# Gate products spread among the steps of an attention, wide products in four more stages, convolution taps moved, weights stored by block

## What is computed

```python
# block 1
z = rms(x, g) @ w_in;  q, k, v, u = split(z)
m = concat(chunked_attention(q, k, v, rel_bias), pool(u)) @ w_o
x = x + rms(m, g2)
up = causal_conv3(rms(x, g3) @ w_up)                   # 2 x 5632 channels, 3 taps
x = x + rms((gelu(up[:5632]) * up[5632:]) @ w_down, g4)
# block 2, with a context of 256 tokens and a condition c
s1, b1, a1, s2, b2, a2 = split(silu(c) @ w_ada + b_ada)   # also for the context
h = rms(x) * (1 + b1) + s1                             # the context the same way
k_a, v_a, k_b, v_b = kv(h and context);  q_a, q_b, g_a, g_b = h @ w_in_2
o_a = attention of 16 heads (4 key heads), q and k normed and rotated
o_b = rms over each of 8 heads of (softmax(q1 k1) - lam * softmax(q2 k2)) v
x = x + a1 * ((sigmoid(g_a) * (o_a @ w_br_a) + sigmoid(g_b) * (o_b @ w_br_b)) @ w_out)
x = x + a2 * ((silu(h2 @ w_ff_gate) * (h2 @ w_ff_up)) @ w_ff_down)
```

## Time and profile before

| | |
|---|---|
| median of 3 runs | 3146.78 us (3143.88 to 3147.21) |
| profiled execution, its own time | 3145.76 us |
| its span, first to last instruction | 3143.9 us |
| granted TensorE clock, mean | 0.97 |
| busy: TensorE, VectorE, ScalarE, GpSimd | 93%, 62%, 50%, 25% |
| weight loads | 1120 of 512 KB, 4.8 us to landing in most stages |
| moved | 598 MB, 190 GB/s over the span |

### The profile page before, as it was taken

How to read it: one execution, slowest core, us unless ns; L and a number is a source line. 1 busy time by engine, 2 the same in 40 slices (tenths; PEclk the granted TensorE clock), 3 DMA queues, 4 the chain that set the end, 5 groups by cost and what they waited for, 6 DMA issues and landing times.

```text
span 3143.9 us, 57610 instructions
## 1 busy us (share of the span) xinstructions
PE 2926.2 (93%) x20282; PEld 2699.2 (86%) x20282; DVE 1946.6 (62%) x2412; ACT 1564.1 (50%) x2203; POOL 786.3 (25%) x646
## 2 busy tenths in 40 slices
PE   7998789999998997999998778999997999999999
PEld 7988789999988997788898547999996888888888
DVE  5566888776688866433456555655766665555554
ACT  5555554345565543323455645665535644334443
POOL 2554432003233321212341402445303400000000
PEclk9999899999999998999998989999998999999999
DMA  7874666657777764344574003887755865656655
GB/s 245 266 246 126 222 201 201 180 181 243 240 225 227 235 218 148 120 149 135 180 248 140 1 1 125 255 261 247 241 182 178 255 213 181 188 186 187 187 185 163
DMA packets 595176, 598.29 MB, mean 190 GB/s; under 512 B 18257, under 2 KB 593105, under 8 KB 594833
## 3 DMA queue, kind: packets, MB, share of 16 engines
q1 hardware_dynamic: 591936, 589.37, 60.3%
q10 hardware_dynamic: 2368, 4.91, 0.4%
q0 software_dynamic: 784, 2.88, 0.3%
HBM read 594.99 MB, written 2.10 MB: 190 GB/s over the span
## 4 chain that ended last, share of the span: by engine, by line
PE 60%; DVE 15%; DMA 10%; ACT 7%; issue 7%; DVEq 1%; ACTq 0%; SPq 0%
PE acc L1334 19%; PE acc L1330 13%; PE acc L1332 13%; PE acc L1333 12%; DVE wlo L850 5%; DMA raw<-w_ada 5%; DMA raw<-w_in 2%; ACT whi L540 2%; ACT cond_products L536 1%; DVE cond_sums L842 1%; DVE conv_out L936 1%; PE sums L1392 1%; DMA raw<-w_up 1%; DMA raw<-w_brb 1%; DVE conv_in L924 1%
## 5 line engine op out<-in xcount | busy, mean ns | idle before, releaser
L850 DVE TENSOR_TENSOR wlo<-raw,whi 128x1024 fp32r<-128x1024 f32 x864 | 1120.3, 1307 | 892.5 <-ACT whi L540 888.9
L1334 PE MATMUL acc<-operand,wlo 128*128 128x256 f32 (+1 forms) x5504 | 1606.6, 292 | 0.0
L540 ACT ACTIVATE whi<-raw 128x1024 fp32r<-128x1024 f32 x864 | 911.3, 1058 | 1096.5 <-PE acc L1334 733.5
L1332 PE MATMUL acc<-operand,whi 128*128 128x256 f32 (+1 forms) x4096 | 1222.6, 298 | 98.3 <-DVE wlo L850 63.4
L1333 PE MATMUL acc<-operand,whi 128*128 128x256 f32 (+1 forms) x4096 | 1210.7, 296 | 0.0
L1334 PEld LDWEIGHTS acc<-operand,wlo 128*128 128x128 f32 x5504 | 1063.0, 193 | 15.4
L1332 PEld LDWEIGHTS acc<-operand,whi 128*128 128x128 f32 x4096 | 795.4, 194 | 125.4 <-DVE wlo L850 56.5
L1333 PEld LDWEIGHTS acc<-operand,whi 128*128 128x128 f32 x4096 | 795.6, 194 | 15.0
L408 POOL TENSOR_TENSOR cond_products<-cond_products 128x512 f32<-128x512 f32 x192 | 252.6, 1316 | 1425.9 <-ACT cond_products L536 1424.0
L1330 PE MATMUL acc<-operand,whi 128*128 128x512 f32 x1408 | 502.9, 402 | 16.9 <-DVE wlo L850 9.0
L536 ACT ACTIVATE cond_products<-raw,cond_silu 128x256 f32<-128x256 f32 x768 | 327.8, 498 | 255.7 <-PE acc L1334 159.3
(11 more groups left out here) (201 smaller groups left out, 2000.0 us busy)
## 6 DMA issues: line engine op xcount, KB each, us to landing
raw<-w_ada SPq DMA_DIRECT2D x256, 512.0 KB, 4.7
raw<-w_in SPq DMA_DIRECT2D x224, 512.0 KB, 4.8
raw<-w_up SPq DMA_DIRECT2D x176, 512.0 KB, 4.8
raw<-w_down SPq DMA_DIRECT2D x88, 512.0 KB, 4.9
raw<-w_fg SPq DMA_DIRECT2D x88, 512.0 KB, 4.3
raw<-w_fu SPq DMA_DIRECT2D x88, 512.0 KB, 4.5
raw<-w_fd SPq DMA_DIRECT2D x88, 512.0 KB, 3.5
raw<-w_o SPq DMA_DIRECT2D x32, 512.0 KB, 4.8
```

Of the source, the lines that this page charges most:

```text
L540: act.activation(whi[j % RING][:], raw[j % RING][:], ACT.Copy).then_inc(hi_done, 2 if st.entries[j % st.upb - 1] == (None, ADA_VEC) else 1)
L850: dve.tensor_tensor(wlo[j % RING][:], raw[j % RING][:], whi[j % RING][:].bitcast(F32), ALU.subtract).then_inc(lo_done, 2 if prev[0] is Non ...
L1332: pe.matmul(out_, h[:, x, f], mov[:, 0], start=first, stop=False)
L1334: ins = pe.matmul(out_, l[:, x, f], mov[:, 0], start=False, stop=last)
```

## The change

It has five parts.

1. **Gates among the attention.** The two gate stages become one, `gates`, of 64 units without items. The norms, attention A and attention B are cut into steps, and slot s of 64 holds gate unit s and the steps due there: norms in slots 0 to 9, attention A from slot 11 (`AT_A`), B from slot 43 (`AT_B`). ScalarE and VectorE prepare unit s+4 in slot s. A gate group accumulates in one bank (`PS[:, 0, gb % 2]`); the other two banks are left to the scores, so that A keeps two score buffers and B, whose step fills both, has one. Sigmoids go to a staging buffer `GT` (in the place of the condition sums), are stored to HBM (`spill`), and are loaded back ahead of the branch stages. The sums and the root of B's output norm move into `branch_a`, behind its first unit, with `output_norm`.
2. **Items** move: `up1b` (split in two, `up1b` and `up1c`) and `out` get four each, the gates none.
3. **Wide form** also in `mix_out`, `down1`, `down2` and `q` stages. In three of them ScalarE first copies the low half into `tiles` (`low_half`), VectorE then adds the high half; in `down2` VectorE adds both.
4. **Convolution.** The newest tap goes to ScalarE (`newest_tap`, Identity with scale and bias from a column), the older ones to `older_taps`, which runs behind the next split.
5. **Layout.** The host stores each matrix by blocks of 256 columns (`by_block`), so that a unit's 4 KB per partition lie in a row.

```diff
-V_STEPS = {"scale": 0, "mix_out": 3, "conv": (6, 9), "down1": 0, "down2": 3, "kv": 0, "q": 0, "gate": 0,
+V_STEPS = {"scale": 0, "mix_out": 3, "conv": (4, 7), "down1": 0, "down2": 4, "kv": 0, "q": 0, "gate": 0,
-A_STEPS = {"conv": (1, 0), "gate": (1, 1), "glu": (2, 1)}
-WIDE = ("glu", "down_x")
+A_STEPS = {"conv": (2, 1), "glu": (2, 1), "mix_out": 1, "down1": 1, "q": 1}
+WIDE = ("glu", "down_x", "mix_out", "down1", "down2", "q")
+LOW_FIRST = ("mix_out", "down1", "q")
...
+    def block_of(w, g, k):
+        return W[w][:, ds(g, 1), k:k + UK, :].rearrange("p g k c -> p (g k) c")
...
-    st_up1b = Stage("up1b", pairs("w_up", "w_up", 4 * GW, DFF + 4 * GW), 2 * n1 - 8, 4, "conv", tile0=8, feat0=8)
+    st_up1b = Stage("up1b", pairs("w_up", "w_up", 4 * GW, DFF + 4 * GW), 8, 4, "conv", ada=1, tile0=8, feat0=8)
+    st_up1c = Stage("up1c", pairs("w_up", "w_up", 8 * GW, DFF + 8 * GW), 2 * n1 - 16, 4, "conv", tile0=16, feat0=16)
-    st_ga = Stage("gate_a", cols("w_in2", 0, KVW + QW, GW), 8, 4, "gate", ada=1, tile0=16)
-    st_gb = Stage("gate_b", cols("w_in2", 0, KVW + QW + D, GW), 8, 4, "gate", ada=1, tile0=48)
+    st_g = Stage("gates", cols("w_in2", 0, KVW + QW, GW), 16, 4, "gate")
-    st_out = Stage("out", cols("out", 0, 0, GW), 8, 4, "out", op=104)
+    st_out = Stage("out", cols("out", 0, 0, GW), 8, 4, "out", ada=1, op=104)
...
+        GT = sb("gate_out", [P, 2, S], F32, place["at"] - 2 * GW * 4)
+        gates = nc.dram_tensor("gates_spilled", (P, 32, S), F32).ap()
+        AT_A, AT_B = 11, 43
...
+            pool.wait_ge(gate_out, 16 * 16)
+            for st in (st_ba, st_bb, st_out, st_u1a):
                 add_condition(st)
...
+            def low_half(st, b, gb):
+                tile = b * (2 * st.GB) + (st.tile0 + 2 * gb)
+                act.wait_ge(used, grouped(st, b, gb))
+                act.activation(R[:, ds(tile if st.kind == "q" else tile + Yt, 2), :], PS[:, gb % 2, :, S:2 * S],
+                               ACT.Copy).then_inc(astep, 1)
...
+            def newest_tap(st, b, gb):
+                act.wait_ge(vstep, vst(st, b, gb, 0))
...
+                for m in range(2):
+                    ins = act.activation(Cb[:, m, :], Zp[:, m, 2:S + 2], ACT.Identity, scale=V[:, ds(t2 + m, 1)],
+                                         bias=V[:, ds(tb + m, 1)])
+                ins.then_inc(astep, 1)
...
+            def norms(s):
+                if s == 0:
+                    head_root(0, 16, 80, NK + 1)
+                if s < 2:
+                    squares(NK + s)
+                elif s < 4:
+                    swap(s - 2)
+                elif s < 8:
+                    swap(NK + s - 4)
+                    squares(NK + s - 2)
+                elif s == 8:
+                    head_root(80, 112, 144, 2 * NK + 1)
...
+            def gate(g):
+                act.wait_ge(used, grouped(st_g, g // 2, g % 2))
+                if g:
+                    act.wait_ge(gate_out, 16 * g)
+                act.activation(GT[:], PS[:, 0, g % 2, :].rearrange("p (a n) -> p a n", a=2),
+                               ACT.Sigmoid).then_inc(evac_done, 1)
+            def spill(g):
+                act.wait_ge(evac_done, group(st_g, 0, g) + 3)
+                act.dma_start(gates[:, 2 * g:2 * g + 2, :], GT[:]).then_inc(gate_out, 16)
+            for s in SLOTS:
+                b, j = divmod(s, st_g.upb)
+                if s < 60:
+                    hi(st_g, b, j + RING, st_g.entries[j])
+                else:
+                    hi(st_ba, 0, s - 60, st_g.entries[j])
+                if s % 4 == 0 and s:
+                    spill(s // 4 - 1)
+                norms(s)
+                attend_a(s + 1 - AT_A)
+                attend_b(s + 1 - AT_B)
+                if s % 4 == 3:
+                    gate(s // 4)
+            spill(15)
             act.wait_ge(b_out, HB)
             act.activation(R[:, 64:72, :], R[:, 40:48, :], ACT.Square).then_inc(o_sq, 1)
...
+                    act.dma_start(R[:, 16 + 8 * c:24 + 8 * c, :], gates[:, 8 * c:8 * c + 8, :]).then_inc(in_ga, 16)
...
                     elif k == "down2":
                         did(dve.tensor_tensor(y, y, sums, ALU.add))
+                        settled()
+                        did(dve.tensor_tensor(y, y, low, ALU.add))
...
+                    if st.kind == "conv" and gb != 0 and (gb == 1 or j - RING == st.last[0] + 1):
+                        older_taps(st, b, gb or 0)
...
+            for s in SLOTS:                      # VectorE
+                b, j = divmod(s, st_g.upb)
+                if s < 60:
+                    lo(st_g, b, j + RING)
+                else:
+                    lo(st_ba, 0, s - 60)
+                norms(s)
+                attend_a(s + 1 - AT_A)
+                attend_b(s + 1 - AT_B)
...
+            dve.wait_ge(in_ga, 32)
             run(st_ba)
+            dve.wait_ge(in_gb, 32)
             run(st_bb)
...
+            def attend_a(n):                     # TensorE
+                if 2 <= n < NA + 2:
+                    m = n - 2
+                    pe.wait_ge(a_prob, m + 1)
+                    if m >= 2:
+                        pe.wait_ge(a_copied, m - 1)
+                    turn(m, scr(m % 2), a_turned)
+                if 3 <= n < NA + 3:
...
+                    values(m, OUTS[h % 2][:, P * b:P * b + P], h // 4, scr(2 + m % 2), a_copied, a_summed)
+                if 0 <= n < NA:
+                    if n == 0:
+                        pe.wait_ge(n_rope, 6)
+                        pe.wait_ge(v2_copied, 12)
+                    score_a(n)
...
+            SUMS_AT = {3: 0, 4: 1, 6: 2, 7: 3, 8: 4, 9: 5}
+            for s in SLOTS:
+                if 2 <= s < 2 + NK:
+                    broadcast(s - 2)
+                if s in SUMS_AT:
+                    head_sums(NK + SUMS_AT[s])
+                attend_a(s - AT_A)
+                attend_b(s - AT_B)
+                b, j = divmod(s, st_g.upb)
+                gb, u = st_g.entries[j]
+                if u == 0:
+                    pe.wait_ge(evac_done, group(st_g, b, gb) + 1)
+                multiply(st_g, b, j, False)
...
+            body(st_ba, 0, insert=0)             # head sums behind its first unit
+            with pe.Fori(1, st_ba.bodies) as b:
+                body(st_ba, b, fresh=False)
...
+    by_block = lambda w: np.ascontiguousarray(
+        w.reshape(w.shape[0] // P, P, w.shape[1] // GW, GW).transpose(1, 2, 0, 3))
```

451 lines of the change are left out of this document (231 added, 220 removed).

## The result

The changed kernel takes 3094.6 us (median of 4 runs, 3092.4 to 3095.2), the kernel before, run beside it, 3145.3 (4 runs, 3136.3 to 3147.2). The ratio is 0.984, 95% interval 0.982 to 0.986. The forecast was 3050, with a range of 3005 to 3095. The median lies at its very edge. Of the 97 us that were to go, 51 did.

A forecast was written before the change was run, and what follows sets the result against it. TensorE's stream of weight products was taken as the bound, but not everywhere. The terms -66 + 5.5 - 7 - 26 + 3 - 6 gave -96.5 on 3145.8 us: 3049, as a median 3050; range 3005 to 3095.

The forecast's parts named there:

- the late swaps: Gate slots 11 to 18: late swap copies bring ScalarE to 47 us against TensorE's 42; 3 us lost.
- The slack of two slots: Attention slots: a turn comes two slots behind its score, so TensorE was not to wait for probabilities.
- Rival 1: Attention slots lock, TensorE waiting for a probability in most of 48, 0.9 us each: +43, 3099; chance 0.13.
- A: Attention and gates in 64 slots, last query to first merge product: 365 us against 431.0, so -66.
- Norms: Slots 0 to 10 of the gates: 53 us of work and 15 of stall, 68 in all.
- The sigmoid: In the second attention's slots, exps behind a sigmoid come some 0.5 us late, four times: 2 us.
- D: Convolution stages, newest taps on ScalarE: 14 bodies gain 2.2 us each, moved items cost 5: -26 (-56 to +17).
- C: Wide form in 168 units of the mixer output, down and query stages: -7 us (-9 to +5).
- B: First branch stage of the merge now holds the head sums and their norm: +5.5 us (0 to +15).
- E: Output stage takes four moved condition items at 0.75 us each: +3 us.
- F: Weight layout by blocks, quicker loads in stretches with items: -6 us (0 to -30).
- Rival 3: Weight loads get slower through the wide pitch of partition rows; at 220 GB/s +253 us, 3303; chance 0.04.

The follow-up runs named there:

- narrow_back: The changed kernel with the wide form undone in all its stages: 3088.9 us, ratio 0.983 to the kernel before.

## Why the prediction fell short

**The step that failed: the late swaps, "3 lost, the rest drawn from the slack".** I had added up ScalarE's work in slots 11 to 18, 47 us, against TensorE's 42, and let 3 us of the difference be lost and the rest be slack. That holds for engines that can run ahead of one another. Here the orders of work closed a loop: VectorE's maximum and normalisation stood behind a split, the split behind a rounding, the rounding behind the swap. The stall was 30 us, not 3, and with the other order alone it is 9. The slack of two slots that I had counted on for probabilities was not there, since the normalisation of a finished exp sat behind the split of the same slot. Rival 1 had the mechanism ("where a late rounding stands before an exp, TensorE waits for a probability"), but spread over all slots at 0.9 us; it acted in ten places, at 0.8 to 9.5 us.

The rest of A came out near, in part by luck. Norms took 69.7 against 68, with stalls in slot 7 for a square (3.74) and in slot 10 for the last rotation (3.20), as named. But TensorE was busy 61.8 of the 69.7 us at a granted clock of 0.89, for work put at 53 at full clock, and waited only 7.9, not 15: the slower products made up for stalls that did not come. A slots were 5.06 rather than 5.42, 11 us better over the stage, B slots 5.71 against 5.8. The sigmoid was put at 0.5 us four times; it cost 1.4 three times and 1.9 once. Behind the last gate product came 7.3 us for a forecast 6.7 (its terms add up to 6.55). In sum 27 + 4 - 11 and small terms is the missing 23.

**A term at nothing: the clock.** The prediction took A's work "at full clock" and expected the clock "near 1.0"; it was 0.94 in the stretch, and in slots 11 to 20 the lower clock made 6.3 us. In D and C it had no term for it either.

**D: the right size for the taps, partly by luck, and the wrong one for the items.** 2.2 a body is what undoing it showed. I had taken it as "nearest to the moved work" of VectorE, but 1.1 of the 2.2 are the clock, of which the prediction says nothing here. The four items in the rest of up 1 were put at 1.3 each, "up to 4.2", by a down stage. They cost 3.0 each in a convolution stage, and 8.2 more through the tree, which I had not looked at. It follows the items in GpSimd's order, so the items pushed it into the taps. I had counted the loads that the items add, and not what the items are moved ahead of on GpSimd.

**C: the added evacuation was not hidden.** "The added evacuations hide behind the stream except at four stage ends" failed in the mixer output alone: a pause of 2.0 us in each of four bodies, 1.2 of it due to the late copy, and about 1 us a body more through the clock. Down 1 and the queries carry items too and lost nothing; why, no run shows. In these and down 2 the wide form brings 6.8 us by `narrow_back`, where the rate alone gives 136 units x 0.055 = 7.5.

**B, E and F held:** +5.7 for +5.5, +4.4 for +3. The layout brought some 8 us for 6, but not by the way given: the DMA share, which was to fall by a fifth, stayed. The 1.3 us that the packets of a load were to take came from the rate of the output store. By the packet times above a load of 512 KB takes 1.7 us of the 16 engines in either layout. Rival 3, a pitch that slows the loads, is refuted: the second up stage moved 243 GB/s where it had 229. The Trainium skill ("DMA: Bandwidth & Descriptors", section "Latency and other measured facts") gives 207 GB/s at a pitch of 512 KiB, 214 when padded, from which the prediction took some 3 us. No such loss shows at the pitches of this kernel, 128 to 786 KB.

The range ended at 3095. The three large errors, the swaps, the tree and the low half, were of one kind: work was called hidden because its engine's busy time left room for it.

## What to carry to other kernels

Where two engines hand work to each other in fixed orders, sum the longest path round the loop, not the busy time of each; put what a third engine waits for (here the maximum and the normalisation) ahead of what has a ring of buffers to spare (the split). Spreading a load out doesn't help in such a loop, and an engine freed by 32 us can be worth little or nothing. When a step is moved, list what now stands behind it on each engine, and look at what the helper engines will be doing beside it. And price a stall of TensorE with the clock: compare its busy time for the same matmuls in both traces. Here that was 6.3 of 23.7 us in the attention slots, 10.7 of 22.0 in the second up stage and 3.9 of 8.0 in the mixer output.

## What was unexpected of the hardware

- Beside GpSimd's passes VectorE's operations on SBUF took two to over five times as long: a split 2.47 us for 1.23, a normalisation 2.58 for 0.49, four taps 8.99 for 1.67. The row maximum, which reads TensorE's sums, kept its 0.68. The Trainium skill, "GPSIMD Engine Reference", section "1. Specifications", says that the two share their way to SBUF and that VectorE's instructions contend if they have two SBUF inputs or run in a 2-port mode. The trace agrees for the split and the taps. The normalisation reads one wide tile; in which mode it ran no run shows.
- 512-column products start 236 or 231.6 ns apart at the same granted clock of 1.00, changing between executions and within one; 11.5 us over the last four stages. Its cause wasn't found.
